# x transposed in memory for all tokens, and six chunks of the first projection in a new order, three of them without the norm factor

## The reference, cut to what matters

```
h = x * rsqrt(mean(x*x) + eps) * g                 # per token; g per channel
[a, g_glu, z] = h @ w_in                           # 1024 x 3072
c = a * sigmoid(g_glu)
y = depthwise causal conv of 31 taps over c
out = (silu(layernorm(y)) * silu(z)) @ w_out
x = x + rmsnorm_post(out)
```

## Time and profile before

| | us |
|---|---|
| median of 3 runs (2240.76 to 2241.32) | 2240.81 |
| the profiled execution | 2241.3 |
| its span | 2239.5 |
| PE busy in the span | 2218.0 (99%) |
| DVE / ACT / POOL busy | 1595.4 / 964.6 / 363.3 |
| granted TensorE clock, mean | 0.999 |

### The profile page before, as it was taken

How to read it: one execution, slowest core, us unless ns; L and a number is a source line. 1 busy time by engine, 2 the same in 40 slices (tenths; PEclk the granted TensorE clock), 3 DMA queues, 4 the chain that set the end, 5 groups by cost and what they waited for, 6 DMA issues and landing times.

```text
span 2239.5 us, 30145 instructions
## 1 busy us (share of the span) xinstructions
PE 2218.0 (99%) x11897; PEld 1951.5 (87%) x11897; DVE 1595.4 (71%) x2019; ACT 964.6 (43%) x1437; POOL 363.3 (16%) x519
## 2 busy tenths in 40 slices
PE   8999999999999999999999999999999999999998
PEld 7788899999888888888888888888889999998887
DVE  6799979997697988999996327852286666667221
ACT  6533333333443225656665115642235656656110
POOL 3111111211121102211210101211112121120000
PEclk9999999999999999999999999999999999999999
DMA  6465566655444313343346435452212333236330
GB/s 221 161 160 152 149 176 175 169 137 166 152 152 166 137 58 99 115 123 112 97 131 232 129 120 207 146 179 87 83 63 89 106 98 106 90 103 239 133 104 29
DMA packets 134030, 299.57 MB, mean 134 GB/s; under 512 B 18945, under 2 KB 55553, under 8 KB 132354
## 3 DMA queue, kind: packets, MB, share of 16 engines
q1 hardware_dynamic: 104866, 198.81, 26.5%
q0 software_dynamic: 29024, 98.83, 15.4%
HBM read 219.21 MB, written 78.75 MB: 133 GB/s over the span
## 4 chain that ended last, share of the span: by engine, by line
PE 59%; DVE 1%; ACT 0%; issue 0%; DMA 0%; SPq 0%; DVEq 0%; ACTq 0%
PE PS L2212 18%; PE PS L2214 18%; PE PS L2213 18%; PE PS L2455 2%; PE PS L2219 1%; PE PS L2218 1%; PE PS L2297 0%; PE PS L2319 0%; DMA rawb<-wb_out_in 0%; PE PS L2460 0%; DVE S1l L1582 0%; DVE S3l L1582 0%; DVE S4r L1967 0%; DVE s7l L1582 0%; PE PS L2306 0%
## 5 line engine op out<-in xcount | busy, mean ns | idle before, releaser
L1633 DVE SCALAR_TENSOR_TENSOR acc<-cp,cw,acc 128x513 f32<-128x513 f32 (+3 forms) x464 | 368.1, 793 | 14.2
L2212 PE MATMUL PS<-HAh,Wh 128*128 128x512 f32 (+3 forms) x968 | 341.9, 353 | 0.2 <-DVE HAl L1582 0.2
L2213 PE MATMUL PS<-HAl,Wh 128*128 128x512 f32 (+3 forms) x968 | 340.2, 351 | 0.0
L2214 PE MATMUL PS<-HAh,Wl 128*128 128x512 f32 (+3 forms) x968 | 340.1, 351 | 0.0
L2212 PE MATMUL PS<-Wbh,s7h 128*128 128x512 f32 x512 | 200.2, 391 | 1.6 <-DVE Wbl L1582 1.0
L2212 PE MATMUL PS<-Vh,HBh 128*128 128x512 f32 x512 | 199.6, 390 | 0.0
L2214 PE MATMUL PS<-Wbh,s7l 128*128 128x512 f32 x512 | 199.3, 389 | 0.0
L2213 PE MATMUL PS<-Wbl,s7h 128*128 128x512 f32 x512 | 199.2, 389 | 0.0
L2214 PE MATMUL PS<-Vh,HBl 128*128 128x512 f32 x512 | 199.2, 389 | 0.0
L2213 PE MATMUL PS<-Vl,HBh 128*128 128x512 f32 x512 | 199.2, 389 | 0.0
L2212 PEld LDWEIGHTS PS<-HAh,Wh 128*128 128x128 f32 x968 | 181.9, 188 | 15.5 <-DVE HAl L1582 0.4
(11 more groups left out here) (245 smaller groups left out, 5227.9 us busy)
## 6 DMA issues: line engine op xcount, KB each, us to landing
raw<-wa_in_in SPq DMA_DIRECT2D x48, 512.0 KB, 3.9
Wl<-wa_in_in POOLq DMA_DIRECT2D x39, 512.0 KB, 5.5
rawv<-wb_v_in SPq DMA_DIRECT2D x64, 256.0 KB, 4.6
QWr<-wb_uz_in SPq DMA_DIRECT2D x64, 256.0 KB, 2.6
v_scratch<-vb POOLq DMA_DIRECT2D x64, 256.0 KB, 2.6
vt<-v_scratch SPq DMA_DIRECT2D x32, 512.0 KB, 3.9
s_scratch<-m POOLq DMA_DIRECT2D x32, 512.0 KB, 4.0
rawb<-wb_out_in SPq DMA_DIRECT2D x28, 512.0 KB, 7.9
```

Of the source, the lines that this page charges most:

```text
L1633: return nc.vector.scalar_tensor_tensor(out=out, in0=src, scalar=w, in1=first, op0=ALU.mult, op1=ALU.add)
L2212: nc.tensor.matmul(out, wh, xh, start=start, stop=False, skip_group_check=seeded)
L2213: nc.tensor.matmul(out, wh, xl, start=False, stop=False, skip_group_check=seeded)
L2214: return nc.tensor.matmul(out, wl, xh, start=False, stop=stop, skip_group_check=seeded)
```

## The change

- The host gives x transposed for all tokens, in two arrays (`x_t0`, `x_t1`), read by rows of 128 channels: row k of columns 0 to 511, of 512 to 1023, and of the second half (`x_row`). The plain tiles are still loaded for the squares, in the order 4 to 7, 0 to 3, 8 to 16.
- Columns 0 to 511 are first split with the gain alone (`first_high`, `first_low`), and the chunks (0,0), (1,0), (2,0) run on them row by row, in the order `FIRST_ROWS`, with no norm factor. The factor of these 512 tokens, spread over partitions in `rnc`, is multiplied onto the three results afterwards on VectorE (`first_factor`, and a product on `cs` after the sigmoid). The columns are then scaled and split again in place for the units from 3 on.
- Columns 512 to 1023 are scaled row by row with the factor in PSUM, and the chunks (0,1) and (1,1) go with them, alternating per row. Then follow (2,1), (3,1), (4,1), (3,0), (4,0), and the plain order.
- The second half is scaled and split one row at units 7 to 14. Factors are spread two tiles after a chunk, from the eighth chunk on; the squares of tiles 8 to 16 stand two ahead of a chunk on ScalarE.
- The transposes of x on TensorE, the spreading of the gain row, the halved first chunk and the weight splits on GpSimd are gone; 12 warming matmuls on zeros stand at the start. Unit 3's weights load into another place (`raw3`).
- The convolution plan of stage A: 6 steps in units 4 and 5, 12 in unit 6, 10 in units 7 to 14, 13 up to 23, 14 in 24 to 34, 13 up to 43, then 9, 12 and 8; before 6, 6, 12 in units 6 to 8, 13 up to 43, 9 and 9. The sum is 521 in both.
- Some pairs of semaphores become one (`ld_hist` and `ld_filters`, `o_g` and `o_g2`, `u_ldv` and `u_gb`, `u_sub` and `u_vom`).

```diff
-        a_order = [(n, c) for c in range(2) for n in range(3)]
-        a_order += [(n, c) for n in range(3, 2 * UNITS_A) for c in range(NCH[n // UNITS_A])]
+        a_order = list(FIRST) + [(3, 1), (4, 1), (3, 0), (4, 0)]
+        a_order += [(n, c) for n in range(5, 2 * UNITS_A) for c in range(NCH[n // UNITS_A])]
...
+            def x_row(k, c):
+                if c == 0:
+                    sp.dma_start(xg[:, k, :], x_t0[k, :, 0:CW]).then_inc(n1_ldk[k], 16)
+                if c == 1:
+                    sp.wait_ge(n1_hi, k + 1)
+                    sp.dma_start(HAr[0][:, k, CW:], x_t0[k, :, CW:]).then_inc(n1_ldk[k], 16)
+                if c == 2:
+                    sp.wait_ge(n1_sq, 8)
+                    sp.wait_ge(n1_sc, k + 1)
+                    sp.dma_start(HAr[1][:, k, :], x_t1[k, :, :]).then_inc(n1_ldk[k], 16)
...
+            sp.dma_start(par[:, :], chan_par).then_inc(ld_con, 16)
             sp.dma_start(con[:, :], consts).then_inc(ld_con, 16)
+            a_load(0)
+            x_row(0, 0)
+            x_row(1, 0)
+            a_load(1)
+            x_row(2, 0)
+            x_row(3, 0)
+            a_load(2)
+            for k in range(4, KD):
+                x_row(k, 0)
+            for t in range(4, 8):
+                x_load(t)
+            for k in range(KD):
+                x_row(k, 1)
+            for t in range(4):
+                x_load(t)
+            a_load(3)
...
             for n in range(2 * UNITS_A):
...
                 if n == 2:
                     c_load(0)
+                    for k in range(2, KD):
+                        x_row(k, 2)
+                    for t in range(11, 15):
+                        x_load(t)
+                if n == 3:
+                    for t in range(15, NTILES):
+                        x_load(t)
...
+            def a_first_chunks():
+                for i, (n, k) in enumerate(FIRST_ROWS):
+                    if k == 0:
+                        pe.wait_ge(a_lo, n + 1)
+                    pe.wait_ge(n1_lo, k + 1)
+                    last = a_row(n, 0, k)
+                    if k == KD - 1:
+                        last.then_inc(a_mm, 1)
+                    if 18 <= i < 22:
+                        if i == 18:
+                            pe.wait_ge(ld_con, 32)
+                        n1_spread(i - 14)
+
+            def a_second_chunks():
+                for k in range(KD):
+                    pe.wait_ge(n1_lo, KD + k + 1)
+                    for n in range(2):
+                        last = a_row(n, 1, k)
+                        if k == KD - 1:
+                            last.then_inc(a_mm, 1)
+                    if k == 5:
+                        for t in range(3):
+                            n1_spread(t)
+                    if k == 6:
+                        n1_spread(3)
...
+                for t in range(8 + 2 * (p - 7), 10 + 2 * (p - 7)):
+                    if p >= 7 and t < NTILES:
+                        n1_spread(t)
...
+            first_factor(0, 1)
+            n1_scale(0, 0)
+            n1_scale(1, 0)
+            a_low(3)
+            n1_low(0, 0)
+            n1_scale(2, 0)
+            dve.wait_ge(a_sig, 1)
+            nc.vector.tensor_tensor(cs[:, 0:CW], cs[:, 0:CW], rnc[:, :], ALU.mult).then_inc(a_norm, 1)
+            n1_low(1, 0)
+            dve.wait_ge(a_norm, 2)
+            a_product(1, 0)
+            n1_scale(3, 0)
+            a_product(1, 1)
+            n1_low(2, 0)
+            first_factor(2, 1)
+            n1_scale(4, 0)
+            n1_low(3, 0)
+            a_low(4)
+            for k in range(5, KD):
+                n1_scale(k, 0)
+                n1_low(k - 1, 0)
+            n1_low(KD - 1, 0)
```

More of the change, by code:

```diff
@@ L211, in build @@
         rc = Region(c_at, m_at)
[L212 to L215, removed]
+        xt = [r(f"xt{i}", [P, D]) for i in range(3)]
+        rnr = r("rnr", [P, WIDTH[1]])
+        rnc = r("rnc", [P, CW])
+        still = r("still", [P, P])
+        r = Region(m_at + 20480, top)
+        raw3 = Region(c_at + 12288, m_at)("raw3", [P, KD, P])
         w_at = r.at
@@ L346, in kp @@
             return ap.rearrange("p k n -> p (k n)")
[L349 to L353, removed]
+        ld_con, ld_filters, c_neg, c_pad = (sem(n) for n in ("ld_con", "ld_filters", "c_neg", "c_pad"))
+        n1_ld = [sem(f"n1_ld{i}") for i in range(4)]
+        n1_ldk = [sem(f"n1_ldk{i}") for i in range(KD)]
+        n1_sq, n1_r, n1_sc, n1_tr, n1_hi, n1_lo, n1_row = (sem(f"n1_{n}") for n in
+            ("sq", "r", "sc", "tr", "hi", "lo", "row"))
+        a_norm = sem("a_norm")
         a_raw = [sem(f"a_raw{i}") for i in range(3)]
@@ L426, in build, with a_turn, a_last @@
             a_free.append((kind, count[kind]))
+        def a_turn(n, c):
+            return NCH[n // UNITS_A] - 1 - c if n in (3, 4) else c
         def a_end(n):
-            return a_pos[n, NCH[n // UNITS_A] - 1] + 1
+            return max(a_pos[n, c] for c in range(NCH[n // UNITS_A])) + 1
+        def a_last(n):
+            return a_free[a_end(n) - 1][1]
         def a_turned(n):
@@ L587, in bi, with x_loads @@
             return t + 8 if t < 8 else t + NTILES
-        def x_loads(slot):
-            return sum(1 for t in range(NTILES) if x_slot(t) == slot)
+        def x_loads(s):
+            return sum(1 for t in range(NTILES) if x_sem(t) == s)
         S7_SLOTS = (0, 2, 1, 2, 0, 1, 0, 1) + (0, 2, 1) * 3
@@ L922, in _ @@
+            for t in range(8, 11):
                 x_load(t)
[L923 to L932, removed]
+            for k in range(2):
+                x_row(k, 2)
@@ L1141, in _ @@
                     z_store(JA * h + j)
+                if 2 <= n < 5:
+                    for t in range(3 * n + 2, 3 * n + 5):
+                        n1_rsqrt(t)
                 y_stores(("A", n))
@@ L1595, in n1_scale_turned @@
-            def n1_scale_turned(t):
-                n, s = rows(t), t % 2
-                dve.wait_ge(n1_ldt[s], 16 * ((t - TURNED) // 2 + 1))
-                dve.wait_ge(n1_tr, t + 1)
-                for k in range(KD):
-                    last = nc.vector.scalar_tensor_tensor(out=xc[s][:, k, 0:n], in0=xc[s][:, k, 0:n],
-                                                          scalar=par[:, P_PRE + k:P_PRE + k + 1],
-                                                          in1=PS[:, 6 + s, 0:n], op0=ALU.mult, op1=ALU.mult)
-                last.then_inc(n1_sc, 1)
@@ new lines, in n1_low, with first_factor @@
+            def n1_low(k, c):
+                dve.wait_ge(n1_hi, (2 * KD, KD, 3 * KD)[c] + k + 1)
+                h, cols = ((0, slice(0, CW)), (0, slice(CW, 2 * CW)), (1, slice(0, WIDTH[1])))[c]
+                split_low(HAl[h][:, k, cols], HAr[h][:, k, cols], HAh[h][:, k, cols], n1_lo)
+            def first_factor(n, count):
+                out = cs if n == 0 else zc
+                dve.wait_ge(n1_row, 1)
+                dve.wait_ge(a_mm, n + 1)
+                nc.vector.tensor_tensor(out[:, 0:CW], PS[:, n, 0:CW], rnc[:, :], ALU.mult).then_inc(a_norm, count)
```

428 lines of the change are left out of this document (216 added, 212 removed).

## The result

The changed kernel takes 2245.13 us (13 runs, 2242.80 to 2247.92) against 2240.81 (13 runs, 2240.21 to 2241.57): a ratio of 1.0018, 95% interval 1.0011 to 1.0025. I had forecast 2229.5. It is 4.3 us slower where 11.3 less were expected, and its runs lie 5 us apart where those of before lie within 1.4.

What follows compares the result with a forecast made beforehand. The matmul engine, busy 2218.0 of 2239.5 us, was taken as the bound. Moving the thirteenth chunk's start from 93.65 to 81.75 saves 11.9, with 0 lost after: 2240.8 - 11.9 = 2228.9, rounded to 2229.5; range 2226 to 2236.

Steps and rivals of the forecast that it cites:

- 0.7 of wait, with 0 and 4.5 as bounds: Before tile 11's spread, after (3,0): its x load queues behind c_load(0) and six x rows, so TensorE waits 0.7 us.
- nothing, 1 as upper bound: Factors 14 to 16 on GpSimd, behind c_store(1): ready at 74.3 and 75.2 for a spread due at 76.1, no wait.
- 2.8: Wait in us before tile 9's spread, after (4,1), through VectorE's catch-up and ScalarE's late squares; range 1.5 to 4.
- mark: First matmul of stage A's thirteenth chunk (unit 6, columns 0 to 511): at 93.65 us before, forecast at 81.75.
- The rate: DMA rate for the x queue: 414 GB/s from the trace; at the skill's 358, tile 11 lands 1.9 us later.
- The low clock: At the start: warming ends near 3.6, 4.5 us without work follow, low level holds to about 13.4; 1.2 us lost.
- The start: First useful matmul at 8.1 us against 17.59, third step at 10.95, first three chunks done at 27.45.
- Second columns: Columns 512 to 1023: a wait of 0.95 us for their scaling and split, phase running 28.4 to 39.35.
- After the mark: Moved convolution steps and merged waits after stage A's thirteenth chunk begins: 0 us lost, upper bound 2.
- (b): Rival, 340 to 484 us: VectorE, 94% busy, cannot follow and the lead is lost; 2237 to 2241 us, chance 0.08.
- (a): Rival: new waits from the cs store, x 11, scaling chain and start; gain 5 to 8, 2233 to 2236, chance 0.20.
- (c): Rival, slower: 20 convolution steps in units 45 and 46 and VectorE's lag exposed; +9.9, 2250.7 us, chance 0.04.

Runs made afterwards that it cites:

- run 1: Changed kernel with each spread of the norm factors of tiles 8 to 16 put two chunks later on TensorE; 2233.4 us, 11.7 less than the changed kernel.
- run 3: Changed kernel with GpSimd computing the factors of tiles 14 to 16 ahead of the store of cs block 1; 3.1 us less.
- run 5: Changed kernel with 20 warming matmul calls at the start instead of 12; 2.6 us less.
- run 2: Changed kernel with matmuls on zeros ahead of the waits for factors 11 (18), 14 (6) and 15 (8); the time did not follow the 3.5 to 4 us expected.
- run 6: Changed kernel with the six second-half x rows issued behind the loads of tiles 11 to 16 on SP; 4.3 us less.
- run 8: Changed kernel with spreads two chunks later, GpSimd's last three factors ahead of the cs store, and 20 warming matmul calls; no gain over run 1.
- run 10: Changed kernel with the later spreads of run 1 and the six x rows last in SP's queue; 2.9 us above run 1.
- run 4: Changed kernel with convolution steps moved from units 45 and 46 to units 7 to 14 (11 each) and 35 to 37 (14 each); 2245.9 us, 0.8 more.
- run 7: Changed kernel with later spreads, factors 14 to 16 ahead of the store, run 4's plan, 20 warming matmul calls and x rows behind the tiles; 2242.5 us.
- run 9: Changed kernel with the later spreads of run 1 and the convolution plan of run 4; 5.6 us above run 1.
- run 11: Run 8 with 14 convolution steps each in units 15 to 36, 10 kept in units 7 to 14, none in 46; 6.5 us more than run 8.

## Why the prediction was wrong

**The steps that failed** are the two that priced the waits in front of the spreads: "0.7 of wait, with 0 and 4.5 as bounds" for tile 11, and "nothing, 1 as upper bound" for factors 14 to 16. Measured: 4.38, just inside its bound (plus 1.07 + 0.71 for tiles 8 and 9, where I had 2.8), and 1.72 + 1.94, far outside. Run 1 takes all of them away and is 11.7 faster. It ends 3.9 above the forecast with its mark where the forecast had it (81.83 for 81.75), and what it loses behind the mark is 4.7.

In the profiled execution the mark is 14.4 late. 2.9 of it were there when (3,0) began (61.76 for 58.9), 3.7 are the wait for tile 11 over its 0.7, 3.7 those for tiles 14 and 15, 2.5 the low clock behind both, and 1.6 small pieces. That run 1 has its mark where the forecast had it is partly luck: its second columns started 2.0 late as well (30.36), and it has none of the 3.5 of wait that the forecast had for tiles 9 and 11.

Tile 11: I let its load stand behind c_load(0) and the rows alone. c_load(0) was issued at 53.66, not 51.4: the store of cs that it waits for was issued at 50.5, behind a gate product at 49.5, and not at about 46.8 (it then landed in 3.1, not 4.5). And the load of tile 11 also waits for the square of tile 8, which came at 58.5 instead of 55.4 as the whole chain was 3 us late; it is then in the queue with the rows, tiles 12 and 13 and the store of zc (512 KB, 9.4 us to land), and takes 10.1 to land. (The prediction's own sum, 3.86 MB at 414 GB/s from 51.4, comes to 60.7 and not to its 61.7; that slip made it later, not earlier.) The rate was nearly right: 389 GB/s from 60 to 70, 406 at the start. The Trainium skill (DMA: Bandwidth & Descriptors, Specifications) gives 358 GB/s, and the trace again passes it with 406. The Trainium skill (HBM Reference, Specifications) says that a core streaming alone measures well above its share of the pair, and that agrees. What failed is the count of what shares the queue and of what the issue waits for.

Factors 14 to 16: I followed GpSimd's queue to the gate product, and took it to be on time. Behind it stood the low part of weights 6, then ScalarE in the square of tile 15. Run 3 shows the last link alone: 3.1.

**The low clock** was priced once (1.2 at the start). At the start it cost 1.7 to 2.6 (run 5: second columns, and time). The warming ended at 6.53 and not near 3.6, as its 12 calls are 24 matmuls; the gap was 2.7 and not 4.5; and the clock did not stay low from the warming on, but was up at 9.23 and down from 10.00 to about 16.8. And it fell again after the waits of 4.4 and 3.7 us: from 72.07 to 74.78 six matmuls took 2.71, against 1.45 from 79.05 to 80.50, and from 88.86 to 91.56 again 2.70. I had priced waits by their length; here the clock added 1.3 to each.

**The start**: 9.23 for 8.1, named as a possible late end; weights 0 were read at 6.11, not 4.95, and the chain behind it took 3.1, as worked out. The third step came at 12.43, not 10.95. With the clock: first chunks done at 30.1, not 27.45. **Second columns**: wait 0.83 for 0.95, right; started 31.11 for 28.4, the same 2.7 late.

**After the mark** I had 0 (upper 2): 2.2 before the output stage, just over the bound, and 1.4 behind 1190, of which the sum knew nothing. The 2.0 near the end of stage A do not depend on the lead: the eight kernels with the changed plan (the changed one and runs 1, 2, 3, 5, 6, 8 and 10) all lose 1.9 to 2.0 there. With the plan of run 4, runs 7 and 9 lose nothing there and run 4 itself 2.8 (the wait of 2.57); run 11, with yet another, loses 6.5. So the plan decides this loss, and my claim that VectorE was level there was wrong by that much; but moving the steps paid nowhere (runs 4, 9, 11), and which steps make the two waits is not shown. Of the lead of run 1, 4.7 were lost, 0.8 of them before 167. That is the effect which my rival (b), "the lead is not kept", described, with 0.08, but not its cause, a VectorE that cannot follow between 340 and 484: the lead of run 1 is 11.0 from 167 to 523.

**The rivals**: (a), a new wait, named the mechanism but let it eat 7 us at most, where 16 went from forecast to result; it had the waits and left out what they do to the clock. (c) had the sign but not the cause. The chance of 0.90 for faster rested on treating these chains as mostly sheltering each other; instead the delay of one was passed on to the next.

**Open**: why the second layer's first weights come late after the change (0.8 to 2.2 us near 1200 in the changed kernel and all eleven runs, none there in before); in run 2 VectorE waits 3.2 us there for the landing of a store of m. Why run 2, with its clock repaired in the profile, gained nothing. And why the same two waits (about 1.06 and 0.71, for tiles 8 and 9) left the clock up in the changed kernel and runs 2, 4 and 5, and brought it down in runs 3 and 6.

## What to carry to other kernels

Place a small operation that needs a late result near its last possible place, not at its first: moving nine spreads by two chunks turned a loss of 4.3 us into a gain of 7.7 with the same work. When pricing a moved load, list all that is in its queue and what its issue waits for, follow each in-order engine to its own head, and add the low clock behind a wait (here 1.3 us more, each time). And test edits together: the plan, which alone cost 0.8, and the rows, which alone gained 4.3, cost 5.6 and 2.9 beside the later spreads.

## What the runs showed of the hardware

- After 12 warming calls (24 matmuls on zeroed operands) the clock of 10 to 17 us was anything from 0.50 (run 4) to 1.00 (run 2); after 20 calls (40 matmuls) it was 1.00 in runs 5, 8 and 11 and 0.76 in run 7. In the changed kernel it was up at the first useful matmul (9.23) and fell at 10.00, in the middle of busy work.
- Clock after waits in these traces: after one of 4.38 us the matmuls ran at 1.2 GHz from 72.07 to 74.78, after 1.72 and 1.94 in a row from 88.86 to 91.56, and after each other single wait of 2.9 to 7.6 us behind the start (runs 3, 4, 5, 7, 9, 11). After waits of 2.57 (run 4) and 2.27 (run 10) they ran at 2.4, after one of 2.20 (run 2) at 1.2 for part of the next 5 us. Waits of 0.5 to 1.2 us near 550 and 563 left the clock up; 1.06 and 0.71 in a row did so in the changed kernel, and brought it down in run 3:

```profile
60.00:70.00 10.00, 7.52 (x26) 5.81 (x26) 5.86 (x8) 4.49 (x8) 1.69 (x4) 0.83 0.91 353
```

- A square of 128x1024 took 1.06 us beside full queues, and its tile (512 KB of x, tiles 11 to 16) 3.5 us to land at the fastest and 10.3 at the slowest.
- GpSimd's small power went from 0.57 to 1.05 us, its 128x1 scaling from 0.22 to 1.17, while VectorE ran its long operations (84.75 to 88.7).
